# A two-block network on one core: matmuls issued ahead of the low halves at the norms, two DMA groups issued elsewhere, x's transposes a tile later, broadcasts with 128 rows

## The chip, the cores and the metric

The kernel runs on one core of one Trainium2 chip. The time is the device time of one execution in microseconds; before the change it is 2996.51 us, the median of three runs (2993.85 to 2999.04). The kernel is one program, written engine by engine: TensorE (PE, with its weight loads shown as PEld), VectorE (DVE), ScalarE (ACT), GpSimd (POOL) and SyncE (SP), which here only issues DMAs. Engines wait for each other through semaphores that the program sets by hand.

## The reference

Everything is float32, batch 1, 512 time steps, width 1024. Two networks of two layers each run one after the other:

```python
def first_block(x, ...):
    for i in range(2):                       # i = 0: SSD mixer, i = 1: RG-LRU mixer
        h = rmsnorm(x, norm_mix_pre[i])
        m = ssd_mixer(h, ...) if i == 0 else rglru_mixer(h, ...)
        x = x + rmsnorm(m, norm_mix_post[i])
        h = rmsnorm(x, norm_ffn_pre[i])
        f = conv_ffn(h, ...)                 # up to 8192, causal conv of 3, gelu(g) * v, down
        x = x + rmsnorm(f, norm_ffn_post[i])

def second_block(x, positions, ...):
    for layer in range(2):                   # 0: HGRN2 + S5, 1: MLA
        hn = rmsnorm_2(h, norm_mix_g[layer])
        mix = even_mixer(hn, ...) if layer == 0 else mla(hn, positions, ...)
        h = h + mix
        h = h + conv_ffn_2(rmsnorm_2(h, norm_ffn_g[layer]), ...)
    return rmsnorm_2(h, final_norm_g)

def ssd_mixer(u, ...):
    z, xbc, dt_raw = split(u @ w_in)         # 2048, 3072, 32 columns
    xbc = silu(causal_dwconv(xbc, conv_w, conv_b))
    dt = softplus(dt_raw + dt_bias)          # 32 heads of 64; chunks of 128 steps
    cs = cumsum(dt * a)                      # within a chunk; scores = (C B^T) * exp(cs_l - cs_s)
    ...                                      # y_diag, states, y_off
    return gated_group_rmsnorm(y, z, norm_w) @ w_out

def s5(u, ...):
    y = ...                                  # diagonal complex states, + d_skip * u
    z = gelu(y)
    return z * sigmoid(z @ w_glu + b_glu)    # 512 wide

def even_mixer(hn, ...):
    return concatenate([hgrn2(...), s5(u, ...)]) @ w_out

def mla(hn, positions, ...):                 # 8 heads, nope 128, rope 64, v 128
    q = rmsnorm_2(cq) @ w_uq; kv = rmsnorm_2(ckv) @ w_ukv
    q_rope, k_rope = rotate(...)
    return softmax(q k^T * scale, causal) v @ w_out
```

## The kernel before, in words

Activations lie transposed: 128 channels on the partitions, the 512 time steps along the free dimension, so that x is eight tiles `xT[:, k, :]`. Every projection runs on PE in `fp32r`, with both operands split in a high and a low half: for each 128x128 block of weights there are three matmuls of 512 columns, whi·h_hi, whi·h_lo and wlo·h_hi (L397 to L399 in `pe_tile`, L419 to L421 in `pe_first`, L871 to L873 for SSD's z). A tile of 128 outputs with 8 blocks is 24 matmuls.

SP streams the raw weights in order of use, in units of usually 128x1024 (`load`, L2552), through a ring of five buffers: a unit's load waits until PE has done the unit five before. ACT makes whi of each unit (L342), POOL makes wlo = raw - whi (L2598). ACT and POOL do this between their other work, each in its written order, so whatever holds up one of them holds up the weights behind it.

**Norms.** A norm before a projection is the class `Pre`: ACT writes h_hi = x * gain (L593), DVE h_lo (L597), ACT squares x, POOL adds the squares up (`nacc`, L542) and PE sums them over the partitions with `ones` (L547, L549); the factor 1/rms is applied at the projection's output. Four such norms (`ffn_pre0`, `norm1`, `ffn_pre1`, `norm2`) directly follow a norm of a mixer's or an FFN's output, their `post`, whose result DVE first scales (L568) and adds (L574); three have none (`ffn_pre2`, `norm3`, `ffn_pre3`). At each, `pe_first` runs the first two or three tiles block by block, because the blocks of h come one by one: for each block it waits for h_lo, and then does the three matmuls of each tile. `ssd_pe` calls it at the start of the kernel, and the LRU's output projection calls it too.

**SSD.** PE projects dt, 24 tiles of xbc and 16 of z. Between the xbc tiles 15 to 22 it transposes the finished x tiles, two per tile (`x_natural`, L855, in pairs). Then come the chunk states (L905), and for each of 16 pairs of heads `decay_rows`: one matmul of 512 columns that broadcasts a row of cumulated sums (L916), the mask (L917), four matmuls of 128 columns (L920), and another broadcast (L934). `cs3` holds the sums split in three parts on 96 partitions.

**S5 and its gate.** After the last S5 matmuls (`s5_out`, L1709) ACT copies four banks to `ysb`, and after each copy issues four DMAs that turn it to `zf` (L1862). DVE adds the skip term (L2072), ACT does the gelu and z_hi, DVE z_lo (L2076). PE then does glu (four tiles of four blocks, L1748 to L1750), ACT the sigmoid, DVE the product, ACT and DVE split it again (L2081), and `ev_out` takes eight tiles of eight blocks, the first four of which are HGRN2's output, the last four S5's.

**MLA.** PE projects the rope parts of q, then q (`uqn`), `uk`, `uv`; the rotated q is laid out by 16 DMAs on SP (`pack_turned`, L2272) that wait for its halves. They stand in SP's list ahead of the load of uk's second unit. `small_stage` (L2249 to L2251) does these tiles; its halves are written by ACT and DVE.

## Time and profile before

| what | before |
|---|---|
| median of 3 runs | 2996.51 us |
| profiled execution, own time | 2994.27 us |
| its span | 2992.5 us |
| mean granted TensorE clock | 0.978 |
| PE busy | 2853.3 us (95%), 13176 matmuls |
| DVE busy | 1297.0 us (43%) |
| ACT busy | 1236.1 us (41%) |
| POOL busy | 1380.7 us (46%) |
| DMA | 256.74 MB, mean 86 GB/s |

Durations of matmuls are modelled and overlap: a 512-column matmul is shown with 0.39 us at full clock and 0.63 at half, but the next one starts earlier than that. So the cost of a matmul is read from the distance between starts, or from a count of them in a stretch. A row of the timeline gives start and length in microseconds, and in brackets how long the engine was idle before it and who released it.

### The profile page before, as it was taken

What the parts mean: (1) busy time and instruction counts of PE and PEld (TensorE: products, weight loads), DVE (VectorE), ACT (ScalarE), POOL (GpSimd) and SP (SyncE); (2) the same over time, 40 slices, a digit from 0 to 9 for tenths busy, and PEclk for the clock granted to TensorE, in tenths of its full rate; (3) what the DMA queues carried; (4) which work ended last, traced back from release to release, by engine and by line L of the source; (5) the groups of instructions that cost most, each with busy time, mean ns of one, the idle gap of its engine ahead of it and who ended that gap; (6) DMA issues with size and microseconds to landing.
All of it is one profiled execution on the core that took longest, in us unless ns stands there. A gap on an engine that the chain in (4) does not pass through costs nothing.

```text
span 2992.5 us, 33154 instructions
## 1 busy us (share of the span) xinstructions
PE 2853.3 (95%) x13176; PEld 2340.7 (78%) x13176; DVE 1297.0 (43%) x1891; ACT 1236.1 (41%) x1746; POOL 1380.7 (46%) x767
## 2 busy tenths in 40 slices
PE   7999999999999899999999999879999988999998
PEld 6777877888888677788888877667888867788886
DVE  5755515531551463653155057734313365343132
ACT  6434436432442673643244244534323335443232
POOL 5333454444444577444444548324444532344443
PEclk9999999999999999999999999889999999999999
DMA  3211122222322223222232332022232321122322
GB/s 134 78 57 50 43 99 85 94 97 99 99 95 96 68 93 96 79 93 98 99 98 94 98 95 88 1 71 92 89 102 96 101 81 61 57 92 89 102 91 85
DMA packets 88024, 256.74 MB, mean 86 GB/s; under 512 B 17344, under 2 KB 21440, under 8 KB 87872
## 3 DMA queue, kind: packets, MB, share of 16 engines
q1 hardware_dynamic: 74288, 249.65, 25.7%
q10 hardware_dynamic: 13584, 4.98, 0.7%
q8 instruction: 105, 1.72, 0.2%
q14 instruction: 47, 0.39, 0.0%
HBM read 248.30 MB, written 2.10 MB: 84 GB/s over the span
## 4 chain that ended last, share of the span: by engine, by line
PE 86%; DVE 6%; ACT 3%; DMA 2%; issue 1%; POOL 1%; SPq 0%; ACTq 0%; POOLq 0%; DVEq 0%
PE bank L397 23%; PE bank L399 23%; PE bank L398 23%; PE bank L419 2%; PE bank L420 2%; PE bank L421 2%; DVE bank L1235 1%; PE bank L871 1%; PE bank L873 1%; PE bank L872 1%; PE bank L953 1%; POOL wlo L2598 1%; PE bank L2339 1%; PE bank L1685 0%; PE bank L549 0%
## 5 line engine op out<-in xcount | busy, mean ns | idle before, releaser
L2598 POOL TENSOR_TENSOR wlo<-raw,whi 128x1024 fp32r<-128x1024 f32 (+2 forms) x497 | 1135.8, 2288 | 1506.3 <-ACT whi L342 1505.4
L342 ACT ACTIVATE whi<-raw 128x1024 fp32r<-128x1024 f32 (+2 forms) x497 | 500.1, 1007 | 1112.3 <-DMA raw<-in_f_up 485.9
L397 PE MATMUL bank<-h_hi,whi 128*128 128x512 f32 x2240 | 879.4, 393 | 11.7 <-DVE h_lo L2081 3.7
L398 PE MATMUL bank<-h_lo,whi 128*128 128x512 f32 x2240 | 873.7, 390 | 0.0
L399 PE MATMUL bank<-h_hi,wlo 128*128 128x512 f32 x2240 | 873.6, 390 | 0.0
L397 PEld LDWEIGHTS bank<-h_hi,whi 128*128 128x128 f32 x2240 | 421.9, 188 | 104.6 <-ACT xbc L1078 5.6
L398 PEld LDWEIGHTS bank<-h_lo,whi 128*128 128x128 f32 x2240 | 422.1, 188 | 89.1 <-issue 1.9
L399 PEld LDWEIGHTS bank<-h_hi,wlo 128*128 128x128 f32 x2240 | 421.8, 188 | 88.2
L397 PE MATMUL bank<-act_hi,whi 128*128 128x512 f32 x864 | 336.2, 389 | 0.9 <-POOL wlo L2598 0.9
L399 PE MATMUL bank<-act_hi,wlo 128*128 128x512 f32 x864 | 336.1, 389 | 0.0
L398 PE MATMUL bank<-act_lo,whi 128*128 128x512 f32 x864 | 336.1, 389 | 0.0
L735 DVE TENSOR_TENSOR tg<-bank,ipre 128x512 f32<-128x512 f32 x108 | 74.6, 691 | 297.3 <-PE bank L399 251.0
L397 PEld LDWEIGHTS bank<-act_hi,whi 128*128 128x128 f32 x864 | 162.2, 188 | 35.1 <-POOL wlo L2598 1.3
L398 PEld LDWEIGHTS bank<-act_lo,whi 128*128 128x128 f32 x864 | 162.2, 188 | 33.8
L399 PEld LDWEIGHTS bank<-act_hi,wlo 128*128 128x128 f32 x864 | 162.2, 188 | 33.5
L691 ACT ACTIVATE bank<-tg,cols 128x512 f32<-128x512 f32 x108 | 84.5, 783 | 116.3 <-DVE tg L735 116.3
L419 PE MATMUL bank<-h_hi,whi 128*128 128x512 f32 x192 | 82.4, 429 | 42.8 <-DVE h_lo L597 41.1
L755 DVE TENSOR_TENSOR xT<-bank,xT 128x512 f32<-128x512 f32 x32 | 22.1, 692 | 190.4 <-PE bank L399 190.4
L740 DVE TENSOR_TENSOR tv<-bank,ipre 128x512 f32<-128x512 f32 x64 | 44.2, 691 | 133.3 <-PE bank L399 133.3
L721 DVE SCALAR_TENSOR_TENSOR bank<-tg,cols,bank 128x511 f32<-128x511 f32 x108 | 81.5, 755 | 30.6 <-ACT bank L691 29.7
L542 POOL TENSOR_TENSOR nacc<-nacc,sqb 128x512 f32<-128x512 f32 x65 | 86.2, 1326 | 16.9 <-ACT sqb L524 16.1
L419 PEld LDWEIGHTS bank<-h_hi,whi 128*128 128x128 f32 x192 | 39.7, 207 | 56.8 <-issue 32.4
(478 smaller groups left out, 3618.0 us busy)
## 6 DMA issues: line engine op xcount, KB each, us to landing
raw<-in_f_up SPq DMA_DIRECT2D x216, 512.0 KB, 3.4
raw<-in_f_dn SPq DMA_DIRECT2D x64, 512.0 KB, 3.4
raw<-in_ssd_xbc SPq DMA_DIRECT2D x24, 512.0 KB, 3.5
raw<-in_f_dn SPq DMA_DIRECT2D x32, 384.0 KB, 3.0
raw<-in_lru_in SPq DMA_DIRECT2D x20, 512.0 KB, 3.4
raw<-in_ev_in SPq DMA_DIRECT2D x20, 512.0 KB, 3.6
raw<-in_f_dn SPq DMA_DIRECT2D x32, 320.0 KB, 2.9
raw<-in_ssd_z SPq DMA_DIRECT2D x16, 512.0 KB, 3.4
```

The source lines that it names most:

```text
L342: act.activation(whi[:, s, 0:WIDTH[u]], raw[:, s, 0:WIDTH[u]], ACT.Copy).then_inc(hi_done, 1)
L397: pe.matmul(out, wh, hi, start=kt == 0, stop=False)
L398: pe.matmul(out, wh, lo, start=False, stop=False)
L399: last = pe.matmul(out, wl, hi, start=False, stop=kt == n - 1)
L419: pe.matmul(out, wh, hi, start=kt == 0, stop=False)
L420: pe.matmul(out, wh, lo, start=False, stop=False)
L421: last = pe.matmul(out, wl, hi, start=False, stop=kt == n - 1)
L542: pool.tensor_tensor(nacc[:], nacc[:], sqb[:, (j + 1) % 2, :], ALU.add).then_inc(s_acc, 1)
L691: act.activation(bg[:], tg[:, e, :], ACT.Identity, bias=self.prm_col(j + prev, 3), scale=self.prm_col(j + prev, 2)).then_inc(self.tap, 1)
L721: dve.scalar_tensor_tensor(out=dst[:, 1:T], in0=src[:, 0:T - 1], scalar=self.prm_col(j + prev, 4 * v + 1), in1=dst[:, 1:T], op0=ALU.mult, ...
L735: dve.tensor_tensor(tg[:, e, :], bg[:], ipre[:], ALU.mult).then_inc(self.u, 1)
L2598: pool.tensor_tensor(wlo[:, s, 0:n], raw[:, s, 0:n], whi[:, s, 0:n].bitcast(F32), ALU.subtract)\
```

## The change

Lines in this section's names are of the kernel before unless said otherwise.

- `pe_first` waits for h_hi of a block, does whi·h_hi and wlo·h_hi of all its tiles, then waits for h_lo and does whi·h_lo of all. Ahead of the first block it issues `spare` matmuls of 512 columns (whi·whi) into the first tile's bank, whose contents the first real matmul overwrites: 17 where the norm has a `post`, 7 where it has none.
- `ssd_pe` issues 20 matmuls of `ones` (128 columns) first; ACT does one tiny activation before its first wait for weights.
- x's transposes stand behind the tiles 16 to 23 instead of 15 to 22; `decay_rows` and `selp` use all 128 partitions.
- ACT copies the four S5 banks one after another; 14 of the 16 DMAs that turn y are issued by SP, ahead of the load of ev_out's fourth unit, and two by ACT. The first four blocks of ev_out's tiles 0 to 2 (36 matmuls) stand between `s5_out` and glu, their last four behind glu. The sigmoid is written in place, the product to other banks.
- The rotated q has other places in memory, `pack_turned` stands ahead of the load of od_out's second unit, and ACT waits for the packed q before uv's tiles and no longer before uk's.

```diff
         def pe_first(pe, tiles, rhs, high_ready, low_ready, spare=0):
             for st, t in tiles:
                 st.pe_start(pe, t)
+            st, t = tiles[0]
+            for n in range(spare):
+                s = (st.u0 + t * st.q) % RING
+                if n == 0:
+                    w(pe, split_done, st.u0 + t * st.q + 1)
+                pe.matmul(st.bank(t)[:], whi[:, s, 0:P], whi[:, s, 0:T], start=True, stop=True)
...
-                ready(kt)
                 hi, lo = rhs(kt)
+                high_ready(kt)
                 for st, t in tiles:
...
-                    pe.matmul(out, wh, hi, start=kt == 0, stop=False)
-                    pe.matmul(out, wh, lo, start=False, stop=False)
-                    last = pe.matmul(out, wl, hi, start=False, stop=kt == n - 1)
+                    pe.matmul(out, whi[:, s, b * P:b * P + P], hi, start=kt == 0, stop=False)
+                    pe.matmul(out, wlo[:, s, b * P:b * P + P], hi, start=False, stop=False)
+                low_ready(kt)
+                for st, t in tiles:
+                    s = (st.u0 + t * st.q + q) % RING
+                    last = pe.matmul(st.bank(t)[:], whi[:, s, b * P:b * P + P], lo, start=False, stop=kt == n - 1)
...
             def pe_first(self, pe, tiles):
-                pe_first(pe, tiles, rhs_h, lambda kt: self.lo_ready(pe, kt))
+                pe_first(pe, tiles, rhs_h, lambda kt: pe.wait_ge(p_hi, self.h0 + kt + 1), lambda kt: self.lo_ready(pe, kt),
+                         17 if self.post else 7)
...
+            pe.wait_ge(consts, 4)
+            for n in range(20):
+                pe.matmul(chunk(stage["ssd_dt"].bank(0), 0), ones[:], ones[:], start=True, stop=True)
...
-                    pe.matmul(bank[4 + e][:], sel3[0:96, h:h + 1].broadcast_to((96, P)), cs3[0:96, :], start=True, stop=False)
+                    pe.matmul(bank[4 + e][:], sel3[:, h:h + 1].broadcast_to((P, P)), cs3[:], start=True, stop=False)
...
-                if 15 <= t <= 22:
-                    x_natural(2 * t - 30)
-                    x_natural(2 * t - 29)
+                if t >= 16:
+                    x_natural(2 * t - 32)
+                    x_natural(2 * t - 31)
...
+            for t in range(3):
+                eo.pe_start(pe, t)
+                pe.wait_ge(split_done, eo.u0 + t + 1)
+                part(t, range(4), (lambda kt: w(pe, n_lo, hnorm[kt].h0 + 1)) if t == 0 else None)
...
+            for t in range(3):
+                part(t, range(4, 8), (lambda kt: w(pe, u_olo, kt - 3)) if t == 0 else None).then_inc(done, 1)
+            for t in range(3, 8):
+                eo.pe_tile(pe, t, rhs_h)
...
             for r in range(4):
                 act.wait_ge(v_y, r + 1)
-                own.link(act.activation(ysb[:, r, :], bank[r][:], ACT.Copy))
-                for a in range(4):
-                    act.dma_start(zf[32 * r:32 * r + 32, :, a * P:a * P + P],
-                                  ysb[32 * a:32 * a + 32, r, :].rearrange("p (j k) -> p j k", j=4)).then_inc(v_u, 16)
+                act.activation(ysb[:, r, :], bank[r][:], ACT.Copy).then_inc(v_cp, 1)
+            act.activation(half[:, 0:1], eps[:], ACT.Gelu_apprx_tanh)
+            act.wait_ge(v_cp, 8)
+            y_back(act, 3, 2)
+            y_back(act, 3, 3)
...
-            act.wait_ge(a_dma, 256)
             halves(stage["uk"], k_hi, 4, T0 + 8)
+            act.wait_ge(a_dma, 256)
...
-                    if (name, k) == ("uk", 1):
+                    if (name, k) == ("od_out", 1):
                         pack_turned(sp)
+                    if (name, k) == ("ev_out", 3):
+                        for r in range(4):
+                            sp.wait_ge(v_cp, 4 + r + 1)
+                            for a in range(4 if r < 3 else 2):
+                                y_back(sp, r, a)
                     load(name, k)
...
+            act.wait_ge(consts, 5)
+            act.activation(rms[:, 0:1], eps[:], ACT.Copy)
             act.wait_ge(c_in, 16)
```

In the order of instructions, PE's between SSD's output and the first FFN, before. L547 and L549 are the sums of squares of the post norm; `p_low` counts h_lo, `split_done` the units that ACT has split.

```order
L547 MATMUL bank<-nacc,ones 128x512 [waits s_rms,s_acc]
L549 MATMUL bank<-sqb,ones 128x512 [waits s_sq]
L419 MATMUL bank<-h_hi,whi 128x512 [waits p_low,bank_free2,split_done,bank_free1,bank_free0]
L420 MATMUL bank<-h_lo,whi 128x512
L421 MATMUL bank<-h_hi,wlo 128x512
L419 MATMUL bank<-h_hi,whi 128x512 [waits split_done]
```

The same place after; the two sums are L555 and L557 there, the fillers L413, and `p_high` counts h_hi.

```order
L555 MATMUL bank<-nacc,ones 128x512 [waits s_rms,s_acc]
L557 MATMUL bank<-sqb,ones 128x512 [waits s_sq]
L413 MATMUL bank<-whi 128x512 [waits bank_free2,split_done,bank_free1,bank_free0]
L413 MATMUL bank<-whi 128x512 x16
L424 MATMUL bank<-h_hi,whi 128x512 [waits split_done,p_high]
L425 MATMUL bank<-h_hi,wlo 128x512
L424 MATMUL bank<-h_hi,whi 128x512 [waits split_done]
L425 MATMUL bank<-h_hi,wlo 128x512
L424 MATMUL bank<-h_hi,whi 128x512 [waits split_done]
L425 MATMUL bank<-h_hi,wlo 128x512
L429 MATMUL bank<-h_lo,whi 128x512 [waits p_low]
L429 MATMUL bank<-h_lo,whi 128x512 x2
```

The three matmuls with h_lo of a block moved behind its six with h_hi, the wait for h_lo with them, and 17 matmuls that need only weights stand in front.

SP's DMAs at MLA, before. `done` counts what PE has finished, `n_lo` and `n_hi` the halves that ACT and DVE wrote.

```order
L2552 DMA raw<-in_uq 128x768 [waits done] x6
L2552 DMA raw<-in_uk 128x1024 [waits done]
L2272 DMA qp<-qr_hi 32x2x512 [waits n_lo,n_hi]
L2272 DMA qp<-qr_hi 32x2x512 x7
L2272 DMA qp<-qr_lo 32x2x512 x8
L2552 DMA raw<-in_uk 128x1024 [waits done]
L2552 DMA raw<-in_uv 128x1024 [waits done] x2
L2552 DMA raw<-in_od_out 128x1024 [waits done] x8
```

After (`load` is L2596, `pack_turned` L2316 there):

```order
L2596 DMA raw<-in_uq 128x768 [waits done] x6
L2596 DMA raw<-in_uk 128x1024 [waits done] x2
L2596 DMA raw<-in_uv 128x1024 [waits done] x2
L2596 DMA raw<-in_od_out 128x1024 [waits done]
L2316 DMA qp<-qr_hi 32x2x512 [waits n_lo,n_hi]
L2316 DMA qp<-qr_hi 32x2x512 x7
L2316 DMA qp<-qr_lo 32x2x512 x8
L2596 DMA raw<-in_od_out 128x1024 [waits done] x7
```

One load of uk, both of uv and the first of od_out now stand ahead of the 16 DMAs.

SP's DMAs between glu's weights and ev_out's, after; before, ten loads stood here in a row and the DMAs that turn y were ACT's. `v_cp` counts ACT's copies.

```order
L2596 DMA raw<-in_glu 128x1024 [waits done] x2
L2596 DMA raw<-in_ev_out 128x1024 [waits done] x3
L1795 DMA zf<-ysb 32x4x128 [waits v_cp]
L1795 DMA zf<-ysb 32x4x128 x3
L1795 DMA zf<-ysb 32x4x128 [waits v_cp]
L1795 DMA zf<-ysb 32x4x128 x3
L1795 DMA zf<-ysb 32x4x128 [waits v_cp]
L1795 DMA zf<-ysb 32x4x128 x3
L1795 DMA zf<-ysb 32x4x128 [waits v_cp]
L1795 DMA zf<-ysb 32x4x128
L2596 DMA raw<-in_ev_out 128x1024 [waits done] x5
```

Fourteen DMAs that each follow a copy of ACT's have come in between the third and the fourth load of ev_out.

## Rows read from the trace of the kernel before

**Rows 1.** The page, part 4: shares of the chain that ended last, by engine.

```profile
PE 86%; DVE 6%; ACT 3%; DMA 2%; issue 1%; POOL 1%; SPq 0%; ACTq 0%; POOLq 0%; DVEq 0%
```

**Rows 2.** Waits of PE: what waits for what, us in total, times, longest.

```profile
PE bank L419 <- DVE h_lo L597: 41.1, 7, 12.7
```

**Rows 3.** PE alone in windows (us, busy (count), granted clock, DMA share, GB/s); one timeline row.

```profile
462.60:466.20 3.60, 3.53 (x9) 0.54 0.00 0
2100.00:2140.00 40.00, 40.00 (x178) 1.00 0.29 96
...
113.57 0.50 PE L397 MATMUL bank<-h_hi,whi 128*128 128x512 f32 x1 [1.54 <-ACT xbc L1078]
```

**Rows 4.** Timeline at norms with a post half, PE, ACT and POOL.

```profile
455.62 1.13 PE L549 MATMUL bank<-sqb,ones 128*128 128x512 f32 x2 [0.59 <-ACT sqb L524]
...
460.94 0.69 ACT L593 ACTIVATE h_hi<-bank,cols 128x512 fp32r<-128x512 f32 x1 [1.56 <-DVE bank L574]
...
462.67 0.76 PE L419 MATMUL bank<-h_hi,whi 128*128 128x512 f32 x1 [5.92 <-DVE h_lo L597]
...
477.85 1.29 POOL L542 TENSOR_TENSOR nacc<-nacc,sqb 128x512 f32<-128x512 f32 x1 [0.36 <-ACT sqb L524]
...
480.62 1.02 PE L547 MATMUL bank<-nacc,ones 128*128 128x512 f32 x2
...
1759.26 1.02 PE L547 MATMUL bank<-nacc,ones 128*128 128x512 f32 x2
```

**Rows 5.** Timeline at ffn_pre2 and norm3, ACT and PE.

```profile
2026.22 5.01 ACT L593 ACTIVATE h_hi<-xT,cols 128x512 fp32r<-128x512 f32 x8 [0.43 <-PE bank L399]
...
2028.52 0.47 PE L419 MATMUL bank<-h_hi,whi 128*128 128x512 f32 x1 [2.34 <-DVE h_lo L597]
...
2391.05 0.39 PE L419 MATMUL bank<-h_hi,whi 128*128 128x512 f32 x1
```

**Rows 6.** Timeline of ACT at the start.

```profile
7.35 1.28 ACT L342 ACT_TABLE_LOAD   x1 [7.35 <-DMA raw<-in_ssd_dt]
```

**Rows 7.** Timeline at x's transposes and before the chunk states.

```profile
124.59 1.94 PE L855 MATMUL bank<-ident,xbc 128*128 128x128 f32 x8 [3.65 <-DVE nat L1224]
...
182.06 1.06 ACT L342 ACTIVATE whi<-raw 128x1024 fp32r<-128x1024 f32 x1 [2.02 <-DMA raw<-in_ssd_z]
...
184.24 3.75 PE L905 MATMUL bank<-xdd,bn 128*128 128x512 f32 x4 [4.38 <-ACT xbc L1074]
```

**Rows 8.** Timeline of PE in decay_rows, and in MLA's scores.

```profile
201.61 0.45 PE L916 MATMUL bank<-cs,sel 96*128 96x512 f32 x1
201.89 0.40 PE L917 MATMUL bank<-mask_r,ident_r 128*128 128x512 f32 x1
202.13 0.56 PE L920 MATMUL bank<-sel,cs 96*128 96x128 f32 x4
202.52 0.45 PE L934 MATMUL bank<-cs,selp 96*128 96x512 f32 x1
...
2501.81 0.27 PE L2320 MATMUL bank<-k_hi,q_lo 128*128 128x128 f32 x1
2501.92 0.28 PE L2321 MATMUL bank<-kp_hi,qp 128*128 128x128 f32 x1
```

**Rows 9.** Timeline around y's DMAs, glu and ev_out, ACT's queue, DVE and PE.

```profile
1956.22 2.55 ACTq L1862 DMA_DIRECT2D zf<-ysb  x4
...
1960.27 2.74 DVE L2072 SCALAR_TENSOR_TENSOR zf<-ev,cols,zf 128x512 f32<-128x512 f32 x4 [11.06 <-DMA zf<-ysb]
...
1963.76 0.77 PE L1748 MATMUL bank<-z_hi,whi 128*128 128x512 f32 x1 [12.45 <-DVE z_lo L2076]
...
1984.85 0.79 PE L397 MATMUL bank<-h_hi,whi 128*128 128x512 f32 x1 [2.96 <-DVE h_lo L2081]
```

**Rows 10.** Timeline at MLA's uk, ACT and PE.

```profile
2472.90 1.06 ACT L342 ACTIVATE whi<-raw 128x1024 fp32r<-128x1024 f32 x1 [12.32 <-DMA raw<-in_uk]
...
2475.22 0.79 PE L2249 MATMUL bank<-ck_hi,whi 128*128 128x512 f32 x1 [9.63 <-DVE q_lo L2502]
```

More of the change, by code:

```diff
@@ L919, in decay_rows @@
                     for c in range(NC):
-                        last = pe.matmul(chunk(bank[4 + e], c), chunk(cs3[0:96, :], c),
-                                         sel3[0:96, 32 + h:33 + h].broadcast_to((96, P)), start=False, stop=c == NC - 1)
+                        last = pe.matmul(chunk(bank[4 + e], c), chunk(cs3[:], c),
+                                         sel3[:, 32 + h:33 + h].broadcast_to((P, P)), start=False, stop=c == NC - 1)
                     last.then_inc(p_cs, 1)
@@ L1737, in even_pe, with part @@
                 s5_out(r)
+            eo = stage["ev_out"]
+            def part(t, kts, ready=None):
+                s = (eo.u0 + t) % RING
+                for kt in kts:
+                    if ready is not None:
+                        ready(kt)
+                    wh, wl = whi[:, s, kt * P:kt * P + P], wlo[:, s, kt * P:kt * P + P]
+                    pe.matmul(eo.bank(t)[:], wh, h_hi[:, kt, :], start=kt == 0, stop=False)
+                    pe.matmul(eo.bank(t)[:], wh, h_lo[:, kt, :], start=False, stop=False)
+                    last = pe.matmul(eo.bank(t)[:], wl, h_hi[:, kt, :], start=False, stop=kt == 7)
+                return last
+            for t in range(3):
+                eo.pe_start(pe, t)
+                pe.wait_ge(split_done, eo.u0 + t + 1)
+                part(t, range(4), (lambda kt: w(pe, n_lo, hnorm[kt].h0 + 1)) if t == 0 else None)
             st = stage["glu"]
@@ L2397, in mla_act @@
             own.link(act.activation(invc[:], bank[7][:, 0:T:P], ACT.Copy))
+            halves(stage["uk"], k_hi, 4, T0 + 8)
             act.wait_ge(a_dma, 256)
-            halves(stage["uk"], k_hi, 4, T0 + 8)
             st = stage["uv"]
```

61 lines of the change are left out of this document (32 added, 29 removed).

## The prediction

> **What bounds the kernel now.** I read the page's head first, then the chain of waits, then PE's waits. PE is busy 95% of a span of 2992.5 us (table above) and the chain that ended last is 86% PE [rows 1]: weights stream in behind it, and only time in which PE stands still or runs slow can be won. In the list of PE's waits the largest is L419 for h_lo: 41.1 us in seven waits, the longest 12.7 [rows 2]. The timeline shows the next two: 12.45 before the glu matmuls for z_lo [rows 9] and 9.63 in MLA's small stage for q_lo [rows 10]. All lie where one stage hands over to the next. Windows show a second price: in the stretch after such a wait the granted clock is 0.54 and nine matmuls begin in 3.4 us, 0.43 apart; in a steady stretch at 1.00 there are 178 in 40 us, 0.225 apart [rows 3]. So the first level is 1.2 GHz, the other 2.4, and each matmul at the lower one costs 0.20 more. The gap of 5.92 [rows 4] was followed by seven of them, the one of 2.34 [rows 5] too; so was the shortest, 1.54 before 113.57 [rows 3].
>
> **The change part by part.** All sums are against the profiled execution, 2994.27 us, 1.8 more than its span and 2.2 below the median of 2996.51.
>
> *Norms with a post half (four).* Now PE ends the sums of squares at 455.62 + 1.13 = 456.75, waits 5.92 for the first h_lo and starts at 462.67 [rows 4]. h_hi(0) is there at 460.94 + 0.69 = 461.63. The change puts 17 fillers (17 x 0.225 = 3.8, to 460.6) in the wait and needs only h_hi to start, at 461.65, 1.0 earlier, at full clock if a gap of 1.0 leaves it. From there ACT gives an h_hi every 2.1 us and nine matmuls take 2.04, so PE goes at ACT's pace. What is late next is POOL: L547 waits for the last nacc, 477.85 + 1.29 = 479.14 [rows 4], which nothing moves. So L547 comes at 479.2 in place of 480.62: 1.4. The fourth such place has the same distances from an L549 1277.39 us later, but its L547 stands at 1759.26 = 481.87 + 1277.39, so 2.65; the middle two stand at 481.40 and 481.56, so 2.2 and 2.35. Sum 8.6; I take 8.5. If the clock does fall in the short gap, 7 matmuls x 0.20 come back each time, down to a sum of 3.2; the fillers themselves wait only for weights and banks that are ready.
>
> *Norms without it (three).* At 2026.22 ACT starts the h_hi, and PE has its first matmul at 2028.52 after a gap of 2.34 [rows 5], with seven slow ones behind (1.4). Seven fillers (1.6) fill it; PE needs h_hi(0) alone, 0.63 from 2026.22. Real work starts at about 2027.8: 0.7 + 1.4 + 0.2 for the h_lo left later = 2.3, at two of the three. At the third PE starts at 2391.05 with no idle time ahead [rows 5]: there the fillers are pure cost, 1.6. Together +4.6 - 1.6.
>
> *Start.* PE's third tile waits for POOL's wlo, which follow ACT's splits, and these begin behind a table load of 1.28 that ACT starts at 7.35, when its first weights have landed [rows 6]. Loading the table before that takes it off the chain: 1.3 (0 if the transfers hold POOL anyway; up to 3.5 if the 20 `ones` matmuls also bring the clock up, some 11 slow matmuls less).
>
> *x transposes.* They wait 3.65 us at 124.59 for DVE's nat [rows 7], with slow matmuls around (6.2 for both, from tile 16's end at 132.6 against 126.3 by cadence + 0.87 of transposes). One tile (24 matmuls, 5.4 us) later nat is there. The pair that is put off to the end costs 0.87, but PE waits 4.38 before L905 at 184.24 for ACT, which waited for a transfer itself [rows 7]: hidden, unless the transfer comes later too. Gain 6.2.
>
> *128 rows.* L916 (96 rows) to L917 (128): starts 201.61 and 201.89, 0.28 apart [rows 8] against 0.225. No row of before shows the same matmul with 128. From one side: the columns stay, 0. From the other: one head takes from L916 at 201.61 to L934 at 202.52, 0.91; two heads and L934 (0.28, as L916) 2.10, where seven full cadences of 0.225 (five matmuls of 512 columns, eight of 128) are 1.58; 0.52 x 16 steps = 8.3. Four chunk matmuls with 96 rows take 202.13 to 202.52, 0.10 each; MLA's 128-column matmuls with 128 rows begin 0.11 apart, at 2501.81 and 2501.92 [rows 8]. They are the nearest row, and alike; so I take only the excess of L916 in some steps, 0.5. By the Trainium skill, TensorE: Matmul & The Clock Gate, section Step-by-step: what each phase is for, loading weights goes by columns and the row count doesn't matter: then 0. By its TensorEngine Tiling (Array Packing), section Key Properties, a change of tiling mode drains the engine; if 96 rows were another mode, each switch to and from L917 would pay, up to the 8.3 above. The 0.28 agrees with a small price at a switch; the 0.10 and 0.11 don't ask for one.
>
> *At no cost.* The LRU's out projection and SSD's first tiles only change order within the same matmuls; Gelu's and Sigmoid's tables load while ACT waits for y; zo and the sigmoid move to banks, whose four ACT operations on the same path stay 512 columns long. If one of these tables came late it would cost 1.3, by the load of [rows 6].
>
> *S5 tail.* ACT copies y four times and issues four DMAs after each, the last four from 1956.22, 2.55 long, 0.64 each; DVE gets the data at 1960.27 and PE starts glu at 1963.76 after 12.45 idle [rows 9]. After: the copies run without issues between, SP starts 14 issues of about 0.64 when the first copy is done, at about 1946.6 (the copies now stand 3.2 apart, the last just before 1956.22: 1956.22 - 3 x 3.2), so the last starts at about 1955.0; ACT has two. DVE starts 3.1 earlier. In the wait PE does 36 matmuls of ev_out (36 x 0.225 = 8.1), work it does later now. Glu starts at about 1960.6 and, at full clock, ends 4.3 earlier. Behind it the second half of ev_out is shorter by 8.1, but covers less: the h_lo of glu's tiles come one by one (2.96 idle at 1984.85 now [rows 9]), and ev_out's fourth load stands behind 14 issues on SP, so ACT's split of it holds up h_hi. I count 0.8, 1.3 and 4.5 of waits and 1.5 of slow matmuls: ev_out ends at 2015.8 against 2026.1, 10.3. Bounds: 6 if glu runs slow and the load is 4 later, 14 with no such wait.
>
> *MLA.* SP issues 16 turned DMAs before load(uk, 1), at 0.64 each as ACT's in [rows 9], 10.2 in all; uk lands, ACT starts its split at 2472.90 after 12.32 idle, PE goes on at 2475.22 after 9.63 [rows 10]. After, uk 1 and both uv are loaded ahead; the 16 start when PE has let go the unit that od_out 0 needs, at the end of the q tiles, 2475.22 - 9.63 = 2465.6, and end at about 2476.0, with od_out 1 behind them, landing at 2479.5 (3.5 from issue to landing, as the page has it for such loads). ACT, in order, takes that split among the uk halves and stands from 2472.6 to 2479.5, so PE waits about 4.8 at 2476.9. I get the scores 7.0 earlier. Bounds: 0 (below), 9.6 (the whole wait).
>
> Sum: 8.5 + 4.6 - 1.6 + 1.3 + 6.2 + 0.5 + 10.3 + 7.0 = 36.8. 2994.3 - 36.8 = 2957.5 for a profiled execution, and 2.2 as before: 2959 to 2960 for the median; I say 2959.
>
> **The rivals.**
> (1) *MLA's wait only moves.* The 16 issues are 10.2 us of SP either way, and SP's next load feeds ACT's next split. If ACT's split of od_out 1 holds uk's halves longer than my 4.8, up to 9.6, PE loses at L2249 what it won. For it: ACT's 12.32 behind one load [rows 10]. Against: two loads more lie ahead. 2959 + 7 = 2966.
> (2) *The clock falls all the same.* In the gaps of 1.0 behind the fillers and before glu: posts 3.2 in place of 8.5, glu 1.4 less. For it: a gap of 1.54 did it [rows 3]; against: these are shorter, and the fillers keep the time before them full. 2959 + 6.7 = 2966. Both (1) and (2): 2973.
> (3) *Rows below 128 are dear.* If the 0.28 of L916 is one end of a drain that the small matmuls pay as well, 7.8 more comes back: 2951. For it speaks L916's 0.28, against it the equal 0.10 and 0.11. The Trainium skill's TensorEngine Tiling (Array Packing), Key Properties, would stand behind it.
> (4) *The other side: the denser PE loses clock.* Filling nearly all of PE's idle time (5% of the span) adds 89 full-width fillers and takes pauses away. The mean granted clock is 0.978 (table above). If the chip answered with a mean 1.3% lower, PE's 2853 us grow by 37 and eat the whole sum; from there on it is slower: 0.978 to 0.965 gives 2996, 0.96 gives 3012. Against it: at full density it grants 1.00 for 40 us with 178 matmuls [rows 3], and 95% busy is dense already.
> (5) *The fillers don't hide.* If ACT or the splits were late, 17 x 4 + 7 x 3 = 89 fillers x 0.225 = 20 us would be the most they can cost, less than the rest gains: 2959 + 8.5 + 4.6 + about 5 = 2977 at worst.
>
> **How the numbers follow.** My forecast 48%; (1) 17%, (2) 14%, both 4%; (3) 9%; (4) 2%; (5) and other mishaps 6%. The range of 8 in 10 runs from 2948 (case 3, or S5 and MLA at their better ends) to 2971 (cases 1 or 2 with some of both). Every case but (4) and a sum of several mishaps lies more than 6 us under 2996.5; 0.2%, 6 us, is about what a measurement here can tell from no change. Faster by more than that 0.97, within 0.01, slower 0.02.
>
> **What the profile of the changed kernel would show.** L424's wait at the four posts is 1.0 and reads h_hi, the clock in the 4 us behind is 1.00, and L555 is ended by POOL's nacc; if it is 0.5, rival 2. Next to L868 no wait for nat. L424 at norm3 starts with seven L413 and no idle before. L1779 waits 1 to 1.5 in place of 12.4, and ACT's L342 in ev_out shows a wait of some 4 for its raw. L2249's equivalent waits about 5; 9 would be rival 1. L916's equivalent 0.23 to its neighbour and y's stage shorter by 9 would be rival 3. A mean clock under 0.97 would be rival 4. I am wrong altogether if PE's idle time falls by less than 20 us.

## The result

| | before | changed |
|---|---|---|
| median | 2995.28 us (4 runs) | 2964.11 us (4 runs, 2962.87 to 2968.15) |
| ratio | | 0.9896 [0.9879, 0.9913] |
| profiled execution, span | 2992.5 us | 2962.1 us (own time 2963.78) |
| mean granted clock | 0.978 | 0.988 |
| PE busy | 2853.3 us (95%) | 2864.8 us (97%) |

The change is 31 us faster where 37 were forecast. One execution more of the changed kernel, in the last submission, took 6352 us with PE busy 99% at a granted clock of 1.00; why isn't known, and it is left out below. The parts of the page that answer to PE's busy time and to [rows 1]:

```profile
PE 2864.8 (97%) x13305; PEld 2345.6 (79%) x13305; DVE 1292.7 (44%) x1891; ACT 1237.4 (42%) x1749; POOL 1381.2 (47%) x767
...
PE 85%; DVE 6%; ACT 4%; DMA 2%; issue 1%; POOL 1%; ACTq 0%; SPq 0%; POOLq 0%; DVEq 0%
```

PE has 129 matmuls more on record: the 89 fillers, and the 20 of `ones`, which are recorded as two each. Its idle time (span less busy) is 97.3 us in place of 139.2; about 20 of these 42 us are filled by fillers (89 x 0.225). PE's waits now (us in total, times, longest), which answer to [rows 2]:

```profile
PE bank L1706 <- ACT cw L1860: 8.8, 1, 8.8
PE bank L424 <- POOL wlo L2647: 6.1, 3, 2.6
PE bank L2293 <- DVE k_lo L2546: 6.1, 2, 5.4
PE bank L396 <- POOL wlo L2647: 6.0, 4, 2.1
PE bank L424 <- ACT h_hi L601: 4.5, 6, 1.0
```

The 41.1 us for h_lo are gone, and 12.4 before glu have become 1.75. In the place of the 41.1 stand 4.5 for h_hi and 6.1 for POOL's wlo. These 6.1 are the three waits at the start of the kernel (2.62, 1.97 and 1.54), where one of 12.7 for h_lo stood. They also show that `split_done` counts POOL's wlo and not, as the section on the change has it, ACT's splits: whoever waits for it waits for POOL. The fillers wait for it too, and at none of the four posts did that hold them. Two more lines are larger: cw (5.64 before) and wlo at L396; k_lo's is dealt with at MLA.

To place the gain I read the same events in both traces and took the difference, and then did so in every experiment. Each number is how much earlier than in the profile of before the event comes.

| event | changed | e1 | e2 | e3 | e4 | e5 | e6 | e7 | e8 | e9 | e10 | e11 |
|---|---|---|---|---|---|---|---|---|---|---|---|---|
| first norm's sums, 34.9 | 1.5 | 1.5 | 1.0 | 0.8 | 1.0 | 1.1 | 0.3 | 1.8 | 0.5 | 0.8 | 0.3 | 0.7 |
| chunk states, 184.2 | 8.1 | 8.0 | 7.6 | 1.1 | 7.4 | 7.5 | 6.8 | 8.5 | 6.9 | 7.3 | 6.8 | 7.2 |
| SSD's post sums, 454.0 | 8.6 | 8.5 | 8.1 | 0.9 | 7.8 | 8.0 | 8.8 | 8.9 | 7.4 | 7.7 | 8.8 | 7.7 |
| sums behind the fourth post, 1759.3 | 17.1 | 11.4 | 15.9 | 9.6 | 16.4 | 16.7 | 17.8 | 18.4 | 15.1 | 12.6 | 17.8 | 15.3 |
| HGRN's transposes, 1857.6 | 13.3 | 11.5 | 14.0 | 5.6 | 12.5 | 12.2 | 15.9 | 13.8 | 15.1 | 8.6 | 15.9 | 15.3 |
| L1692 (cw), 1919.6 | 15.3 | 8.8 | 11.3 | 4.1 | 10.4 | 12.7 | 13.2 | 14.1 | 12.9 | 7.2 | 13.3 | 14.2 |
| glu, 1963.8 | 16.6 | 12.2 | 14.2 | 7.2 | 11.4 | 15.0 | 15.5 | 16.4 | 14.4 | 9.9 | 12.8 | 16.3 |
| sums behind ffn_pre2, 2046.6 | 27.6 | 22.4 | 24.3 | 17.3 | 20.8 | 21.2 | 26.4 | 26.2 | 23.6 | 20.1 | 22.8 | 26.7 |
| sums behind norm3, 2407.4 | 26.0 | 22.4 | 24.4 | 15.7 | 19.2 | 19.6 | 24.8 | 24.6 | 22.0 | 18.6 | 21.2 | 26.7 |
| last q matmuls, 2464.3 | 24.3 | 20.6 | 22.0 | 14.9 | 19.1 | 19.6 | 23.9 | 24.4 | 21.5 | 17.9 | 20.6 | 24.9 |
| scores, 2501.6 | 27.9 | 23.7 | 25.9 | 18.9 | 22.8 | 23.1 | 23.6 | 28.7 | 25.1 | 24.6 | 24.5 | 31.4 |
| end, 2979.1 | 30.5 | 25.1 | 27.3 | 20.2 | 23.7 | 24.4 | 26.6 | 31.1 | 26.5 | 27.5 | 25.6 | 34.1 |

Read down a column, a step between two rows is what that stage gained; along a row, all kernels with the same code in a stage show how far chance alone moves it. Between the fourth post and HGRN the changed kernel gives back 3.8; e3, e4, e5, e7 and e9 give back 3.9 to 4.5, e2, e6 and e10 1.9, and e1, e8 and e11 nothing. That was not in the sum.

**The posts.** Timeline of the changed kernel at the first of them, and a window behind it:

```profile
447.58 4.46 PE L413 MATMUL bank<-whi 128*128 128x512 f32 x17
...
453.08 0.50 PE L424 MATMUL bank<-h_hi,whi 128*128 128x512 f32 x1 [1.04 <-ACT h_hi L601]
...
469.26 1.29 POOL L550 TENSOR_TENSOR nacc<-nacc,sqb 128x512 f32<-128x512 f32 x1 [0.38 <-ACT sqb L532]
...
470.60 1.13 PE L555 MATMUL bank<-nacc,ones 128*128 128x512 f32 x2
```

```profile
453.00:457.00 4.00, 3.92 (x17) 3.12 (x18) 3.83 (x6) 2.12 (x5) 0.00 (x0) 1.00 0.00 0
```

The gap is 1.04 in place of 5.92 [rows 4], 17 matmuls begin in 4 us at a granted clock of 1.00 where nine began in 3.6 at 0.54 [rows 3], and the sums wait for POOL's last nacc (469.26 + 1.29). The same holds at the other three.

**The S5 tail.** SP's and ACT's DMA issues, DVE, PE and ACT, in the order of [rows 9]:

```profile
1932.42 9.75 SPq L1795 DMA_DIRECT2D zf<-ysb  x14
...
1943.66 2.74 DVE L2115 SCALAR_TENSOR_TENSOR zf<-ev,cols,zf 128x512 f32<-128x512 f32 x4 [8.57 <-DMA zf<-ysb]
...
1947.15 0.47 PE L1779 MATMUL bank<-z_hi,whi 128*128 128x512 f32 x1 [1.75 <-DVE z_lo L2119]
...
1957.37 1.06 ACT L341 ACTIVATE whi<-raw 128x1024 fp32r<-128x1024 f32 x1 [2.91 <-DMA raw<-in_ev_out]
...
1963.02 1.06 ACT L341 ACTIVATE whi<-raw 128x1024 fp32r<-128x1024 f32 x1 [2.49 <-DMA raw<-in_ev_out]
...
1965.34 0.79 PE L1760 MATMUL bank<-h_hi,whi 128*128 128x512 f32 x1 [3.10 <-DVE h_lo L2124]
...
1971.79 1.06 ACT L341 ACTIVATE whi<-raw 128x1024 fp32r<-128x1024 f32 x1 [6.74 <-DMA raw<-in_ev_out]
```

Glu starts at full clock after 1.75. Behind it PE waits 0.49, 0.62 and 3.10, in all 4.2, where 0.8, 1.3 and 4.5 were counted. The load that the prediction feared is not what it waits for: SP's 14 issues end at 1942.17, and ev_out's fourth load is issued only at 1953.80, when PE lets its unit go, 17.6 us earlier than before (1971.38). The 3.10 follows ACT's split of the fifth unit (2.49 of waiting), which stands ahead of the last two h_hi; the kernel before had 2.96 at the same place. ACT's long wait of 6.74 comes behind all h_hi, and no wait of PE follows it.

**MLA**, ACT and PE at uk and at the scores, against [rows 10]:

```profile
2447.45 0.50 PE L2293 MATMUL bank<-ck_hi,whi 128*128 128x512 f32 x1 [0.68 <-DVE k_lo L2546]
...
2456.27 1.06 ACT L341 ACTIVATE whi<-raw 128x1024 fp32r<-128x1024 f32 x1 [6.44 <-DMA raw<-in_od_out]
...
2458.59 0.80 PE L2293 MATMUL bank<-whi,ck_hi 128*128 128x512 f32 x1 [5.38 <-DVE k_lo L2546]
...
2473.67 0.30 PE L2362 MATMUL bank<-k_hi,q_hi 128*128 128x128 f32 x1 [1.54 <-ACT vT L2447]
```

The wait stands in the middle of uk, for the split of od_out's second unit, as the prediction had it. It is 6.1 in two pieces (0.68 and 5.38) and not 4.8, and some 10 slow matmuls (2.0) follow it, which the sum had left out.

### The profile page after: what moved, and what is told of

Read it like the earlier page. It is cut to its first block, busy times and chain, and to the rows that moved or that the text cites. A ratio compares the mean times of both kernels' runs of the same rounds, so it can differ in the third digit from the quotient of the medians.

```text
span 2962.1 us, 33424 instructions
## 1 busy us (share of the span) xinstructions
PE 2864.8 (97%) x13305; PEld 2345.6 (79%) x13305; DVE 1292.7 (44%) x1891; ACT 1237.4 (42%) x1749; POOL 1381.2 (47%) x767
## 4 chain that ended last, share of the span: by engine, by line
PE 85%; DVE 6%; ACT 4%; DMA 2%; issue 1%; POOL 1%; ACTq 0%; SPq 0%; POOLq 0%; DVEq 0%
PE bank L396 23%; PE bank L397 23%; PE bank L398 23%; PE bank L424 1%; PE bank L429 1%; PE bank L425 1%; PE bank L884 1%; PE bank L885 1%; PE bank L886 1%; POOL wlo L2647 1%; PE bank L967 1%; DVE bank L1249 1%; PE bank L2383 1%; ACT whi L341 1%; ACT h_hi L601 0%
## 5 line engine op out<-in xcount | busy, mean ns | idle before, releaser
L396 PE MATMUL bank<-h_hi,whi 128*128 128x512 f32 x2216 | 868.6, 392 | 10.2 <-ACT xbc L1092 3.7
L398 PE MATMUL bank<-h_hi,wlo 128*128 128x512 f32 x2216 | 863.3, 390 | 0.0
L397 PE MATMUL bank<-h_lo,whi 128*128 128x512 f32 x2216 | 863.2, 390 | 0.0
L396 PEld LDWEIGHTS bank<-h_hi,whi 128*128 128x128 f32 x2216 | 416.9, 188 | 101.5 <-ACT xbc L1092 5.5
L396 PE MATMUL bank<-act_hi,whi 128*128 128x512 f32 x864 | 336.2, 389 | 0.9 <-POOL wlo L2647 0.9
L396 PEld LDWEIGHTS bank<-act_hi,whi 128*128 128x128 f32 x864 | 162.2, 188 | 35.0 <-POOL wlo L2647 1.3
L398 PEld LDWEIGHTS bank<-act_hi,wlo 128*128 128x128 f32 x864 | 162.2, 188 | 33.9
L424 PE MATMUL bank<-h_hi,whi 128*128 128x512 f32 x192 | 78.0, 406 | 10.9 <-POOL wlo L2647 6.1
L734 DVE SCALAR_TENSOR_TENSOR bank<-tg,cols,bank 128x510 f32<-128x510 f32 x108 | 81.4, 754 | 3.9
```

Of the source, the lines that this page charges most:

```text
L396: pe.matmul(out, wh, hi, start=kt == 0, stop=False)
L397: pe.matmul(out, wh, lo, start=False, stop=False)
L398: last = pe.matmul(out, wl, hi, start=False, stop=kt == n - 1)
L424: pe.matmul(out, whi[:, s, b * P:b * P + P], hi, start=kt == 0, stop=False)
L734: dve.scalar_tensor_tensor(out=dst[:, 2:T], in0=src[:, 0:T - 2], scalar=self.prm_col(j + prev, 4 * v), in1=dst[:, 2:T], op0=ALU.mult, op1= ...
```

## The experiments

All are edits of the changed kernel. Times of different submissions come from different chips, so single stages are read from the table above. Of the slower kernels only e3's ratio to before lies clear of the changed kernel's interval [0.9879, 0.9913]; what the others' edits are worth rests on their stages alone.

**e1_no_fill**

```diff
-                         17 if self.post else 7)
+                         0)
```

> The changed kernel with no filler matmuls at the seven norms; the order with h_hi first stays. Theory (the fillers keep the clock): at the four norms with a post half the gap before the first L424 is 4.9 us in place of 1.0, 7 to 13 matmuls behind it run 0.43 apart, and the sums of squares come 1.3 to 2.5 later each, 5 to 10 us in all. At the two norms behind a residual a gap of some 0.8 remains, too short to cost the clock, so real work starts 0.8 earlier, and at norm3 1.6 earlier: 3.2 back. Net 2 to 7 us slower than the changed kernel. Rival (the order alone does it, PE catches up behind ACT's pace before POOL's last sum): nothing is lost at the posts, and the kernel is 3 us faster than the changed one.

Measured: 2968.86 us (2967.77 to 2970.39), ratio to before 0.9917 [0.99, 0.9933]. At the posts:

```profile
453.39 0.77 PE L424 MATMUL bank<-h_hi,whi 128*128 128x512 f32 x1 [5.14 <-ACT h_hi L601]
...
2007.70 0.47 PE L424 MATMUL bank<-h_hi,whi 128*128 128x512 f32 x1 [1.01 <-ACT h_hi L601]
```

```profile
453.30:457.30 4.00, 3.91 (x11) 0.58 0.00 0
```

With the same early start the clock is at its lower level again and eleven matmuls begin in 4 us. The four posts win 0.8 + 0.5 + 0.7 + 2.0 = 4.0 (from the sums before each to those behind it) where the changed kernel wins 1.4 + 2.2 + 2.6 + 2.7 = 8.9: the order alone is worth 4, the fillers 4.9, a little under the 5 to 10 expected. At the two norms without a post half the order alone leaves a gap of 1.0 without slow matmuls, as expected. Counted from the last matmul ahead of the norm (fillers aside) to its sums, e1 wins 2.9 at each, and every kernel with the seven fillers wins 2.6: real work is 0.3 earlier without them, not 0.8. At norm3 nothing is lost. That e1 wins only 1.3 from the scores to the end, where the changed kernel wins 2.6, has another cause, in code that both share. In od_out PE waits 1.41 for an h_lo, in both:

```profile
2541.36 0.50 PE L396 MATMUL bank<-h_hi,whi 128*128 128x512 f32 x1 [1.41 <-DVE h_lo L2569]
```

```profile
2545.43 0.67 PE L396 MATMUL bank<-h_hi,whi 128*128 128x512 f32 x1 [1.41 <-DVE h_lo L2569]
2545.90 0.63 PE L397 MATMUL bank<-h_lo,whi 128*128 128x512 f32 x1
```

In the changed kernel (first) the matmuls behind it go on at full clock; in e1 (second) eight last 0.63 or a little more. The rival, that the order alone does it, falls.

**e2_norm3**

```diff
-                         17 if self.post else 7)
+                         17 if self.post else 0 if self is norm3 else 7)
```

> The changed kernel with no fillers at norm3 alone, the norm at which PE had no idle time before. Theory: seven matmuls less, 1.6 us earlier from the sums of squares behind norm3's first tiles on; a time within 2 us of the changed kernel's. Rival (they hold the clock or hide in a wait there too): nothing moves at that place.

Measured: 2966.07 us (2959.41 to 2967.0), 0.9893 [0.9879, 0.9908]. Over norm3 the events stay where they were (24.3 and 24.4) where the changed kernel loses 1.6 (27.6 and 26.0). The seven fillers there are pure cost, as every other column with them shows too. The kernel's time doesn't tell 1.6.

**e3_x15**

```diff
-                if t >= 16:
-                    x_natural(2 * t - 32)
-                    x_natural(2 * t - 31)
+                if 15 <= t <= 22:
+                    x_natural(2 * t - 30)
+                    x_natural(2 * t - 29)
```

> The changed kernel with x's transposes behind tiles 15 to 22 again. Theory: the wait of 3.65 for nat at tile 15 and the slow matmuls behind it return, 6.2 us, of which the wait before the chunk states gives about nothing back: 5 to 6.5 us slower. Rival (the pair put off to the end costs what is won, or the 128 rows brought the gain): under 2 us slower.

Measured: 2976.53 us (2974.1 to 2976.74), 0.994 [0.9926, 0.9955]: 12 us over the changed kernel's, twice what was expected. Up to the chunk states, counted from the first norm, it wins 0.3 where the changed kernel wins 6.6 (8.10 - 1.45), so the stage itself is worth 6.4, as expected. Another 0.7 comes right behind it, where the wait before the states is 4.42 in e3 and 3.42 in the changed kernel, so that 7.1 go with the edit. The rest of the 10.3 by which its profile ends later arises in code that is the same: 0.6 at the start, and 3.5 in S5's first part (to cw), where the clock differs (below), of which 1.7 come back before glu, and 1.3 behind the scores, at that gap of 1.41. I can't tie these to the edit.

**e4_rows96**: the operands of the three broadcasts, and `selp`, back to `[0:96]`.

> The changed kernel with the broadcasts on 96 rows again. Theory: the distance from L916's equivalent to the mask returns to 0.28 from 0.23, once in several steps; 0.5 us slower over the stage, within 2 us of the changed kernel. Rival (a switch to fewer rows drains the engine each time): 8 us slower, with the step of two heads at 2.1 in place of 1.6.

Measured: 2968.01 us (2967.02 to 2970.56), 0.9915 [0.99, 0.993]. One head of the changed kernel (128 rows) and of e4:

```profile
192.64 0.45 PE L930 MATMUL bank<-cs,sel 128*128 128x512 f32 x1
192.93 0.39 PE L931 MATMUL bank<-mask_r,ident_r 128*128 128x512 f32 x1
193.15 0.55 PE L934 MATMUL bank<-sel,cs 128*128 128x128 f32 x4
193.54 0.46 PE L948 MATMUL bank<-cs,selp 128*128 128x512 f32 x1
```

```profile
203.27 0.45 PE L930 MATMUL bank<-cs,sel 96*128 96x512 f32 x1
203.55 0.40 PE L931 MATMUL bank<-mask_r,ident_r 128*128 128x512 f32 x1
203.79 0.56 PE L934 MATMUL bank<-sel,cs 96*128 96x128 f32 x4
204.18 0.45 PE L948 MATMUL bank<-cs,selp 96*128 96x512 f32 x1
```

0.90 and 0.91 for a head, [rows 8] had 0.91; the first matmul keeps its 0.29 with 128 rows. Over three groups of heads (239.86 to 374.58) the changed kernel wins 0.1 and e4 0.0. The rows are worth nothing here. That also disposes of the drain as rival: 96 and 128 rows alternate here without a price. The rule on modes in the Trainium skill, TensorEngine Tiling (Array Packing), section Key Properties, is thus not seen at work between these matmuls; the one that weight loads go by columns alone (TensorE: Matmul & The Clock Gate, section Step-by-step: what each phase is for) agrees with the trace, where those of the broadcasts last 0.19 us with 96 rows and with 128. e4's profile ends 6.8 later than the changed kernel's, all of it in code that is the same: mainly 4.2 in S5's first part (-2.1 to cw where the changed kernel has +2.0), 1.6 between glu and the next sums, and 1.6 behind the scores, less 1.5 that it wins back at q.

**e5_nopart**

```diff
-            for t in range(3):
-                eo.pe_start(pe, t)
-                pe.wait_ge(split_done, eo.u0 + t + 1)
-                part(t, range(4), ...)
...
-                part(t, range(4, 8), ...).then_inc(done, 1)
+            for t in range(8):
+                eo.pe_tile(pe, t, rhs_h, ...)
```

> The changed kernel with all of ev_out behind glu again (the y DMAs stay on SP, the sigmoid in place). Theory: the wait before glu is about 9.9 in place of 1.75 and some 7 slow matmuls follow it; of the 8.1 us of matmuls put back behind glu, up to 3 hide in the waits that stand there now. Between glu's start and the next norm's sums the kernel is 6 us slower and glu starts as it did, in all 5 to 8 us slower. Rival (the waits behind glu are the bound, so the early part only moved them): under 2 us slower.

Measured: 2969.43 us (2968.19 to 2971.51), 0.991 [0.9895, 0.9925].

```profile
1948.77 0.76 PE L1775 MATMUL bank<-z_hi,whi 128*128 128x512 f32 x1 [9.75 <-DVE z_lo L2113]
1949.33 0.63 PE L1776 MATMUL bank<-z_lo,whi 128*128 128x512 f32 x1
```

The wait is 9.75, seven matmuls last 0.63 behind it, and the stretch from glu to the next norm's sums wins 6.2 against 9.2 to 11.0 in the kernels with the early part: so the early part is worth 3 to 5 of the 8.1 + 1.4 that went with the wait, and the rest came back, in part as waits: 4.2 and seven slow matmuls behind glu in the changed kernel, 2.1 and none in e5. Expected were 5 to 8, too many.

**e10_yact**: ACT issues the 16 DMAs, four behind each copy.

> The changed kernel with the 16 DMAs that turn y issued by ACT again, four behind each of its copies; ev_out's early part stays. Theory: the copies stand 3.2 apart again, so DVE and with it glu start about 3 us later, with the wait before glu 4.5 to 5 in place of 1.75 and the clock down behind it (1.4 more); ev_out's fourth load is no longer held by SP, but PE's waits behind glu are for DVE's halves, which move along. 3 to 5 us slower at ev_out's end. Rival (the early load pays for the late glu): under 1 us.

Measured: 2967.82 us (2967.57 to 2968.72), 0.9909 [0.9894, 0.9924]. From cw to glu it loses 0.4 where the others win 1.1 to 3.4 (the changed kernel 1.3); glu waits 4.92 for z_lo. That makes 1.5 to 3.8, and 2.7 against the middle of the others, under or at the lower edge of the 3 to 5 expected; its rival (under 1) falls. Behind glu it wins 9.9, within the others' 9.2 to 11.0, so the loss stays. ACT's waits for ev_out's loads are as in the changed kernel:

```profile
1967.01 1.06 ACT L341 ACTIVATE whi<-raw 128x1024 fp32r<-128x1024 f32 x1 [2.08 <-DMA raw<-in_ev_out]
...
1975.81 1.06 ACT L341 ACTIVATE whi<-raw 128x1024 fp32r<-128x1024 f32 x1 [6.78 <-DMA raw<-in_ev_out]
```

Here no y DMA stands on SP ahead of the fourth load, and the long wait is 6.78 all the same. So SP's issues never held that load, and an earlier load was not what stood to be won there.

**e6_mla_old**: `pack_turned` ahead of uk's second load, ACT's wait ahead of uk's halves.

> The changed kernel with the 16 turned DMAs ahead of uk's second load and ACT's wait ahead of uk's halves, as before; the new places in memory stay. Theory: the one wait of 9.6 with some 10 slow matmuls (2.0) returns in place of the changed kernel's 0.7 and 5.4 with 10 slow: 3.5 us slower between the end of the q tiles and the scores. Rival (the wait only moved, and what differs is the clock): within 1 us.

Measured: 2971.26 us (2967.62 to 2972.98), 0.9923 [0.9908, 0.9938]. The wait of 9.6 is back, and from the last q matmuls to the scores it loses 0.3 where the changed kernel wins 3.6: the move is worth 3.9, by the other kernels with the changed kernel's code there (3.2 to 4.0) 3.4 to 4.3.

**e7_pack0** and **e9_split**

```diff
-                    if (name, k) == ("od_out", 1):
-                        pack_turned(sp)
+                    if (name, k) == ("od_out", 0):      # e7
+                        pack_turned(sp)
+                    if name == "od_out" and k < 2:      # e9: k = 0 qr_hi's eight, k = 1 qr_lo's
+                        pack_turned(sp, k)
```

> The changed kernel with the 16 turned DMAs ahead of the load of od_out's first unit in place of its second. Theory (what holds PE 5.4 us in uk is SP: its 16 issues of 0.64 stand ahead of the load that ACT splits among uk's halves): SP starts them some 6 us earlier, od_out's second unit lands by the time that ACT comes to it, the wait of 5.4 and its 10 slow matmuls (2.0) go, and the scores come 5 to 7.5 us earlier. Rival (ACT or DVE is late by itself, or the wait goes to od_out's first load, which ACT splits at the first half of uk): under 2 us.

> The changed kernel with the 16 turned DMAs in two groups: the eight of qr_hi ahead of od_out's first load, the eight of qr_lo ahead of its second. Theory (each of the two loads may be issued as soon as PE lets its unit go, 2440.7 and 2446.8 in the changed kernel's trace, and eight issues of 0.64 fit before each): neither load is late, the waits of 5.4 (changed kernel) and 6.7 (e7_pack0) shrink to under 1.5 with no slow matmuls behind, and the scores come 6 to 7.5 us earlier than in the changed kernel, counted from the last q matmul. Rival (something else ends the wait, DVE's halves or the packed DMAs' traffic): under 3 us.

Measured: e7 2965.44 us (2963.18 to 2968.34), 0.9899 [0.9883, 0.9916]; e9 2964.03 us (2962.1 to 2966.78), 0.9896 [0.9882, 0.9911]. PE's wait and what ACT waits for, in e7:

```profile
2450.86 1.06 ACT L341 ACTIVATE whi<-raw 128x1024 fp32r<-128x1024 f32 x1 [7.35 <-DMA raw<-in_od_out]
...
2453.38 0.79 PE L2293 MATMUL bank<-ck_hi,whi 128*128 128x512 f32 x1 [6.74 <-DVE k_lo L2546]
```

and in e9:

```profile
2454.53 1.06 ACT L341 ACTIVATE whi<-raw 128x1024 fp32r<-128x1024 f32 x1 [4.54 <-DMA raw<-in_od_out]
...
2457.05 0.50 PE L2293 MATMUL bank<-ck_hi,whi 128*128 128x512 f32 x1 [3.90 <-DVE k_lo L2546]
```

e7's theory falls to its rival: the wait went to od_out's first load, and from q to the scores it wins 4.2, 0.6 more than the changed kernel. Split in two, the issues leave 3.9 of it, and the stage wins 6.7, 3.1 more than the changed kernel and half of what was expected. What is left has another cause in each. In e7 PE begins q's last matmul at 2440.35, and the load is issued at 2445.82, when SP is through with its 16 issues. In e9 SP's eight issues fit, as planned, and the load is issued 0.45 us behind q's last matmul, as in the changed kernel (0.43); e9's row first, then the changed kernel's:

```profile
2447.31 0.59 SPq L2596 DMA_DIRECT2D raw<-in_od_out  x1
```

```profile
2440.88 0.33 SPq L2596 DMA_DIRECT2D raw<-in_od_out  x1
```

But ACT gets it at 2454.53, 7.2 later, and in the changed kernel 4.0 later (2444.90). The difference is that in e9 it shares the queue's transfers with qr_hi's eight DMAs ahead and qr_lo's eight behind it. So the rival named for e9, the packed DMAs' traffic, took the other half; that these DMAs slow the load is argued from the order, no run moves them away.

**e8_late**

```diff
             for e in range(2):
-                ...                                   # act.dma_start of s5_b and s5_c, ahead of the tiles
             for t in range(20):
                 st.split_ahead(t)
+                if t in (0, 1):
+                    e = t
+                    act.dma_start(braw[rows], dram["s5_b"][rows, :, :, cols16]).then_inc(v_in, 16)
+                    act.dma_start(ccp[0][rows], dram["s5_c"][rows, :, :, cols16]).then_inc(v_in, 16)
```

> The changed kernel with ACT's four DMAs of S5 parameters (L1805, L1806) behind its first two splits of ev_in's units instead of ahead of them. Theory (ACT's issues take 8.3 us there in place of 5.5 before the change, since SP's loads fall beside them, and ACT's splits and POOL's wlo behind them are late): the new wait of 2.1 at PE's sixth tile of ev_in and the seven slow matmuls (1.4) go, and HGRN's first transposes come 3.5 us earlier. Rival (POOL or the loads themselves are late): under 1 us at that place. The S5 part behind it differs by 4 us from run to run with the clock.

Measured: 2964.83 us (2960.18 to 2967.79), 0.9893 [0.9878, 0.9907]. ACT's issues and PE's wait in the changed kernel:

```profile
1744.90 0.65 ACTq L1805 DMA_DIRECT2D braw<-in_s_b  x1
1745.59 3.24 ACTq L1806 DMA_DIRECT2D ccp<-in_s_c  x1
1748.85 1.26 ACTq L1805 DMA_DIRECT2D braw<-in_s_b  x1
1750.14 3.14 ACTq L1806 DMA_DIRECT2D ccp<-in_s_c  x1
1753.55 1.99 ACT L341 ACTIVATE whi<-raw 128x1024 fp32r<-128x1024 f32 x2
...
1757.19 0.76 PE L396 MATMUL bank<-h_hi,whi 128*128 128x512 f32 x1 [2.14 <-POOL wlo L2647]
```

and the same four in the kernel before, where PE had no such wait:

```profile
1761.90 0.65 ACTq L1764 DMA_DIRECT2D braw<-in_s_b  x1
1762.58 2.46 ACTq L1765 DMA_DIRECT2D ccp<-in_s_c  x1
1765.07 1.25 ACTq L1764 DMA_DIRECT2D braw<-in_s_b  x1
1766.35 1.17 ACTq L1765 DMA_DIRECT2D ccp<-in_s_c  x1
```

In e8 the wait is gone and the stage to HGRN's transposes gives nothing back (15.1 and 15.1) where the changed kernel gives back 3.8; 3.5 were expected. The cause is shown: ACT issues four DMAs ahead of the split, and the split reaches PE late. e1 says the same from the other side: its four issues happen to take 6.1 us, its first split comes 9.1 behind the fourth post's sums in place of 11.4, and it gives nothing back. Why the issues take 8.3 us and not 5.5 is argued only, though all thirteen profiles fit: the fourth issue took 2.75 to 3.49 us in the eleven where it began 0.5 to 0.8 behind SP's fourth load of ev_in, and 1.17 and 1.28 in the kernel before and e1, where it began 0.31 ahead of that load and 0.18 behind it. PE's wait is 1.95 to 2.04 in e2, e6 and e10, with no slow matmul behind, and 2.11 to 2.61 in the six others with this code, with seven or eight: hence their 1.9 and 3.8 to 4.5.

**e11_all** and **after_again**: e2, e8 and e9 together, and the changed kernel once more.

> The changed kernel with three edits of this study together: no fillers at norm3, ACT's four parameter DMAs behind its first two splits of ev_in, and the turned DMAs in two groups. By the parts: 1.6 + 3.6 + 6.5 = 11.7 us faster than the changed kernel if nothing is given back, about 2953; under 2960 in any case if two of the three hold.

> The changed kernel itself once more, as the measure for e11_all on the same chip. 2964, and in the trace the S5 part either at the lower clock (as before and e4_rows96) or the higher.

Measured on one chip: e11 2958.80 us (2955.01 to 2961.51), 0.9876 [0.9859, 0.9892]; the changed kernel 2961.80, 2963.08 and 2965.08. So e11 is about 4.3 us faster by the medians of four and three runs, all its runs below all of the other's (2961.51 against 2961.80 at the closest), and the fastest kernel here; 11.7 were expected. The profiled execution of `after_again` is the one left out above, so it has no column in the table. Its parts hold in the table: nothing lost from the fourth post to HGRN (15.3 and 15.3), nothing at norm3 (26.7 and 26.7), 6.5 from q to the scores. That is 3.8 + 1.6 + 2.9 = 8.3 over the profile of the changed kernel; its own profile is 3.7 better, since it gained 0.8 less at the start, 0.8 less in the LRU and 3.2 less in S5's first part, where nothing was edited.

## Why the prediction was right, and where it was off

Added up as measured, the named terms give 8.9 + 5.3 - 1.6 + 1.4 + 6.6 + 0 + 9.7 + 3.6 = 33.9 where the sum had 36.8. The profile ends 30.5 earlier: 3.8 was left out of the sum, and 0.4 came by chance.

**The posts** (8.5): 8.9, by the mechanism named. Without fillers they win 4.0, so "down to a sum of 3.2" was about what a fallen clock costs. Rival 2's gap of 1.0 never lowered the clock.

**The norms without a post half** (+4.6 - 1.6): ffn_pre2 and ffn_pre3 win 2.6 each, in all eleven profiles with fillers there, and norm3 loses 1.6, as e2 shows.

**The start** (1.3): 1.45 in this profile, but 0.3 to 1.8 over the twelve of the changed kernel and its edits. The table load now runs ahead of the weights' landing, and ACT's first split starts at 7.34 in place of 8.64, 1.3 earlier. What the 20 `ones` matmuls add was not tested apart.

**x's transposes** (6.2): 6.6; e3 gives 6.4. The pair that was put off is hidden: the wait before the states is 3.42 where it was 4.38 [rows 7].

**128 rows** (0.5): nothing. The 0.28 of [rows 8] was no price of the rows; rival 3 falls.

**S5 tail** (10.3): about right, but in part by luck. From cw to behind ffn_pre2 the profile wins 12.3, of which 2.6 are the norm's: 9.7. Three things in the working don't stand. Its own terms (4.3 + 8.1 less 6.6 and 1.5, plus the 0.71, 2.96 and seven slow matmuls that stood there before) come to about 9.4. Glu was to start 3.1 earlier, and counted from cw it starts 1.3 earlier (1.1 to 3.4 over the profiles that have the move). And the 4.5 for a load held behind SP's 14 issues named a wait that doesn't exist; 3.10 stood there, for the reason that gave 2.96 before. As to what brought the 9.7: without the early part (e5) 5.9 of it are left, with ACT's issues (e10) 6.9. The two edits overlap, and their worths of 3.8 and 2.8 don't add up to the whole: the other 3.1 are kept by either one alone. The sigmoid in place was not tested apart.

**MLA** (7.0): 3.6, the term that was mis-sized; e6 gives 3.9. The step "so PE waits about 4.8" measured 6.1, and no slow matmuls were counted behind a wait of that length (2.0), though [rows 3, 4] say that they follow. Rival 1 was half right: the wait moved, and was 8.1 with its slow part where it had been 11.5.

**Left out**: the 3.8 between the fourth post and HGRN. "At no cost" looked at matmul order and tables; it did not ask what a faster first stage of ev_in meets. Counted from the fourth post's sums, ACT's first split of ev_in came at 11.4 us in place of 8.5, behind its DMA issues, and PE, itself 2.7 sooner, stood for it: what the fourth post had won was given back at once (e8).

**Chance**: against the other profiles, that of the changed kernel was lucky by some 4 us in S5 and by 1.4 in od_out (at the gap of 1.41), and unlucky by 1.7 at q. Windows of PE over the same 64-column matmuls, before and changed:

```profile
1907.00:1914.00 7.00, 6.98 (x34) 0.50 0.01 2
```

```profile
1891.50:1895.50 4.00, 3.99 (x37) 1.00 0.00 0
```

Both come behind the same short waits (0.97 and 1.38, in all thirteen traces). Only the changed kernel's, e5's and e7's have this group at the upper level throughout (31 matmuls begin in 3.4 us), e4's and e8's for most of it, the other eight at the lower (6.4). Up to cw the changed kernel wins 2.0, e5 and e7 0.5 and 0.3, and the others lose 1.2 to 2.7. This is chance and not the edits: the changed kernel, e2, e5, e6, e7, e9 and e10 are the same code up to this place, and three of these seven have the upper level throughout and four the lower. Rival 4 goes the other way: the mean clock rose from 0.978 to 0.988.
